# The first norm of a two-block fp32 kernel: two weight units interleaved three tiles apart, and the sum of squares moved to GpSimd

## The reference

```python
def rmsnorm(x, g):
    xf = x.astype(jnp.float32)
    y = xf * lax.rsqrt(jnp.mean(xf * xf, axis=-1, keepdims=True) + NORM_EPS)
    return (y * g.astype(jnp.float32)).astype(x.dtype)
...
h = rmsnorm(x, g_pre)
proj = h @ w_in
u, q, k, v, o, gi, gf, ga, gb = jnp.split(proj, IN_SPLITS, axis=-1)
y_a = jax.nn.gelu(s5_ssm(u, lam_re, lam_im, b_re, b_im, c_re, c_im, d, log_dt))
```

## Time and profile before

| what | value |
|---|---|
| median of 3 runs | 1600.15 us (1598.99 to 1601.24) |
| the profiled execution's own time | 1595.28 us |
| span in the profile, first to last instruction | 1593.1 us |
| mean granted TensorE clock | 0.978 of full speed |
| TensorE busy | 1501.2 us, 94% |
| VectorE busy | 856.4 us, 54% |
| ScalarE busy | 619.7 us, 39% |
| GpSimd busy | 290.2 us, 18% |

### The profile page before, as it was taken

The page is one execution under the profiler, slowest core; times in us unless marked ns, Lnnn a source line. Parts: engine busy times, 40 slices in busy tenths (PEclk is TensorE's granted clock), DMA queues, the critical chain, the costliest instruction groups (busy, mean ns, idle before and its releaser), DMA issues.

```text
span 1593.1 us, 23438 instructions
## 1 busy us (share of the span) xinstructions
PE 1501.2 (94%) x9205; PEld 1294.8 (81%) x9205; DVE 856.4 (54%) x1252; ACT 619.7 (39%) x916; POOL 290.2 (18%) x284
## 2 busy tenths in 40 slices
PE   7698999999979999999996989999979999999998
PEld 7697999999968988988984767887767788888887
DVE  6869744457465443543556446767553533434354
ACT  5447656642243221231234235555452423223130
POOL 2934100000045513631534000000010000000000
PEclk9899999999989999999998999999899999999999
DMA  5121212124202232232231211111112222323221
GB/s 187 54 68 53 68 54 67 54 80 147 93 27 94 92 106 82 91 105 93 89 110 53 93 40 54 41 41 40 40 53 80 88 98 93 105 82 104 93 93 66
DMA packets 35493, 126.17 MB, mean 79 GB/s; under 512 B 4396, under 2 KB 4524, under 8 KB 35280
## 3 DMA queue, kind: packets, MB, share of 16 engines
q1 hardware_dynamic: 33888, 120.09, 22.7%
q10 hardware_dynamic: 864, 4.33, 0.7%
q0 software_dynamic: 656, 0.56, 0.1%
HBM read 122.84 MB, written 2.10 MB: 78 GB/s over the span
## 4 chain that ended last, share of the span: by engine, by line
PE 86%; DVE 8%; ACT 3%; issue 2%; POOL 2%; DMA 0%; SPq 0%; DVEq 0%; ACTq 0%; POOLq 0%
PE ps L1573 72%; PE ps L1903 2%; PE ps L1593 2%; PE ps L1929 2%; PE ps L1751 1%; PE ps L1916 1%; PE ps L1701 1%; PE ps L1884 1%; DVE w_lo L778 1%; PE ps L1634 1%; DVE b_tmp L781 1%; POOL acc L1440 1%; POOL conv_tmp L1531 1%; DVE sq L790 1%; POOL gate_conv L1440 0%
## 5 line engine op out<-in xcount | busy, mean ns | idle before, releaser
L1573 PE MATMUL ps<-h_hi,w_hi 128*128 128x264 f32 (+1 forms) x1792 | 525.0, 342 | 35.2 <-DVE h_lo L790 24.8
L1573 PE MATMUL ps<-h_lo,w_hi 128*128 128x264 f32 (+1 forms) x1792 | 504.9, 330 | 0.0
L1573 PE MATMUL ps<-h_hi,w_lo 128*128 128x264 f32 (+1 forms) x1792 | 503.6, 330 | 0.0
L778 DVE TENSOR_TENSOR w_lo<-w_raw,w_hi 128x1024 fp32r<-128x1024 f32 x223 | 289.7, 1299 | 184.1 <-ACT w_hi L325 182.9
L1573 PEld LDWEIGHTS ps<-h_hi,w_hi 128*128 128x128 f32 x1792 | 306.3, 189 | 84.3 <-issue 36.5
L1573 PEld LDWEIGHTS ps<-h_lo,w_hi 128*128 128x128 f32 x1792 | 303.2, 189 | 36.6 <-issue 7.7
L1573 PEld LDWEIGHTS ps<-h_hi,w_lo 128*128 128x128 f32 x1792 | 303.0, 189 | 31.3
L325 ACT ACTIVATE w_hi<-w_raw 128x1024 fp32r<-128x1024 f32 x223 | 232.8, 1051 | 229.2 <-PE ps L1573 228.2
L1573 PE MATMUL ps<-mlp_lo,w_hi 128*128 128x512 f32 x256 | 100.9, 394 | 0.0
L1573 PE MATMUL ps<-mlp_hi,w_hi 128*128 128x512 f32 x256 | 100.3, 392 | 0.0
L1573 PE MATMUL ps<-mlp_hi,w_lo 128*128 128x512 f32 x256 | 99.4, 388 | 0.0
(11 more groups left out here) (283 smaller groups left out, 1939.1 us busy)
## 6 DMA issues: line engine op xcount, KB each, us to landing
w_raw<-w_units SPq DMA_DIRECT2D x223, 512.0 KB, 3.7
x<-x_t ACTq DMA_DIRECT2D x1, 2112.0 KB, 8.1
out<-out_tile SPq DMA_DIRECT2D x8, 256.0 KB, 2.0
x<-x_t ACTq DMA_DIRECT2D x3, 528.0 KB, 9.1
x<-x_t ACTq DMA_DIRECT2D x2, 264.0 KB, 4.5
dil<-dil POOLq DMA_DIRECT2D x1, 512.0 KB, 3.6
consts<-consts SPq DMA_DIRECT2D x1, 320.0 KB, 6.9
b_step<-ssm_b SPq DMA_DIRECT2D x1, 256.0 KB, 10.5
```

Source lines behind the costliest of these rows:

```text
L778: Dv.do(v.tensor_tensor(wlo[:, s % RING, :], raw[:, s % RING, :], f32(whi[:, s % RING, :]), ALU.subtract), lo_ready)
L1573: ins = mm(o, wt[:, s % RING, w], xt[:, kx, c0:c0 + n], start=(b == 0 and a == 0), stop=(b == len(blocks) - 1 and a == 2))
```

## The change

1. Norm 0 moves from the first kind to the second: `PRE, POST` become `(2, 4, 5), (0, 1, 3)`. ACT's `entry_square` writes tile 0's square to `acc`, the others to `sq`, and from tile 3 on waits for POOL's addition of tile m - 2. POOL runs `post_norm(0, T1)` after its clearing and before the small load's scaling; it ends there after six additions. TensorE makes two column sums after the units in place of eight between the blocks.
2. Unit 1 is split after tile 2 and not after tile 5, on ACT and on DVE.
3. TensorE runs units 0 and 1 together: the blocks of unit 1 follow those of unit 0 at a distance of `ENTRY_LAG = 3` tiles. In the order of the program: unit 0 on tiles 0, 1, 2, 3, unit 1 on tile 0, unit 0 on tile 4, unit 1 on tile 1, and so on to unit 0 on tile 7 and unit 1 on tiles 4 to 7; then the two column sums.
4. The counts of the other norms are adapted (a term of `y_scaled` is lowered by one norm).

```diff
-PRE, POST = (0, 2, 4, 5), (1, 3)
+ENTRY_LAG = 3
+PRE, POST = (2, 4, 5), (0, 1, 3)
...
+            def entry_square(m, src):
+                if m >= 3:
+                    act.wait_ge(sem("sq_added"), m - 2)
+                A.do(dn.activation(sq[m % 2][:, :] if m else acc[:, :], src, ACT.Square), sem("sq_ready"))
...
-                tile_square(0, m, x[:, m, :])
-                if m == 5:
+                entry_square(m, x[:, m, :])
+                if m == 2:
                     split_hi(1)
...
-                if m == 5:
+                if m == 2:
                     split_lo(1)
...
+                if norm == 0:
+                    return
                 pool.wait_ge(sem("rs_ready"), norm + 1)
...
             Po.do(g.memset(c_pow[:, :, :, :, :], 0.0), sem("zeros"))
+            post_norm(0, T1)
             pool.wait_ge(sem("ssm_c_in"), 16)
...
+            def block_of(s, xhi, xlo, outs, k):
+                for a, (wt, xt) in enumerate(((whi, xhi), (whi, xlo), (wlo, xhi))):
+                    for o, c0, n in outs:
+                        ins = mm(o, wt[:, s % RING, k * P:k * P + P], xt[:, k, c0:c0 + n], start=(k == 0 and a == 0),
+                                 stop=(k == KT - 1 and a == 2))
+                return ins
+
+            def two_units(s, outs, ready, base, lag, after):
+                begin(s)
+                for k in range(KT + lag):
+                    if k < KT:
+                        pe.wait_ge(ready, base + k + 1)
+                        ins = block_of(s, hhi, hlo, outs[0], k)
+                        if k == KT - 1:
+                            ins.then_inc(unit_done, 1)
+                        after(k)
+                    if k == lag:
+                        begin(s + 1)
+                    if k >= lag:
+                        ins = block_of(s + 1, hhi, hlo, outs[1], k - lag)
+                        if k - lag == KT - 1:
+                            ins.then_inc(unit_done, 1)
...
             for n in range(U_GLU):
-                begin(n)
+                if n > 1:
+                    begin(n)
                 if n == 0:
-                    unit(n, 0, hhi, hlo, halves(n), sem("h1_lo"), after=lambda b: tile_sum(0, T1, b))
-                else:
+                    two_units(0, (halves(0), halves(1)), sem("h1_lo"), 0, ENTRY_LAG, lambda k: None)
+                    post_stat(0, T1)
+                elif n > 1:
                     unit(n, 0, hhi, hlo, halves(n))
```

More of the change, by code:

```diff
@@ L1143, in residual @@
                         else:
-                            dve.wait_ge(sem("y_scaled"), (KT - OWN_SCALED) * POST.index(norm) + m - OWN_SCALED + 1)
+                            dve.wait_ge(sem("y_scaled"), (KT - OWN_SCALED) * (POST.index(norm) - 1) + m - OWN_SCALED + 1)
                         stt(x[:, m, c0:T1], ysum[:, m, 0:n], col(gain, m), x[:, m, c0:T1], M, A_, sem(ready))
```

## The result

The changed kernel took 1606.76 us, the median of 20 runs, beside 1599.15 us for the kernel before in runs of the same kind. The medians are 7.6 us apart; the ratio, estimated from all undisturbed runs and not from the two medians, is 1.0038 with a 95% interval of 1.0025 to 1.0051: slower by 6.1 us (4.0 to 8.2). One of the 20 runs of before took 5250.62 us, which its median hardly feels. I had forecast 2.4 us, from the one start of `rs`. That start did become late, and by more than 2.4 us. But in the medians and in the profiled execution there is a second part, far from the change, that the prediction does not contain.

A forecast was written before the change was run, and what follows sets the result against it. The prediction took the chain through DVE from the first `rs` operation as the bound, with TensorE slack behind it. `rs` moves from 24.25 to 26.7 us, giving 1600.15 + 2.4 = 1602.5 us; range 1599.8 to 1606.0 us.

The forecast's parts named there:

- TensorE has slack from 24 to 69 us, and one start decides: Entry to transposes: the chain runs through DVE and ACT, so only the first `rs` operation's start, 24.25 us, matters.
- rival 2: Between 24 and 69 us: TensorE sets the pace, so units done earlier make it 3.3 us faster; chance 0.05.
- unit 1's blocks, which nobody needed yet, stand ahead of the sums: TensorE before `rs`: six saved sums, 5.4 us, are spent on unit 1's blocks, 5.8 us; alone +0.5 us.
- the lower bound: Entry: if `hlo` of tiles 4 to 7 always comes in time, `rs` starts at 25.55 us, 1.3 us later.
- the feed: Entry: DVE's `hlo` supply to TensorE, slowed by GpSimd's additions taking turns, puts `rs` at 26.7 us, +2.4 us.
- pitch of 1.76 us: Entry, tiles 4 to 7: one GpSimd addition and one `hlo` together take 1.76 us, read from norm 1.
- complete turns of 2.08 us: Entry: addition and `hlo` never overlap, 2.08 us a pair, putting `rs` at 28.0 us, +3.7 us.
- the term before it: Entry, before the turns: tile 3's `hlo` runs without an addition beside it, 0.77 us, and is there at 14.2 us.
- rival 1: Entry: the feed is slower still or TensorE's clock falls in the new pause; +3.2 to +4.1 us, chance 0.20.
- a delay has nothing to be lost in: From `rs` to the kernel's end: each step waits for the one before, so the full +2.4 us reach the end.

The follow-up runs named there:

- e3: Changed kernel with the two column sums moved ahead of unit 1's blocks on tiles 4 to 7; ratio to the kernel before 1.0016.
- e4: Changed kernel with GpSimd's six additions cut to one column of 528; ratio to the kernel before 1.0032.
- e5: Kernel before with only units 0 and 1 interleaved and unit 1 split at tile 2, column sums still between blocks on TensorE; ratio 1.0045.
- e6: Kernel before with only the squares added on GpSimd, units in old order, and unit 1 split after tile 7 instead of tile 5; ratio 1.0002.
- e12: Changed kernel with ten unused matmuls filling TensorE's pause before unit 0's block on tile 3; ratio to the kernel before 1.0065.
- e9: Changed kernel run once more unaltered, as control for the runs with a delay; median 1607.74 us, ratio to the kernel before 1.0066.
- e11: Changed kernel with four extra DVE multiplications, 3.0 us of delay, behind the first norm's factor; median 1603.64 us, ratio to the kernel before 1.0032.
- e7: Changed kernel with two extra DVE multiplications, 1.5 us of delay, behind the first norm's factor; median 1601.34 us, ratio to the kernel before 1.0027.
- e10: Repeat of e7, the changed kernel with 1.5 us of delay; median 1602.44 us, ratio to the kernel before 1.0031.
- e1: Kernel before with five extra DVE multiplications, some 3.7 us of pure delay, behind the first norm's factor; ratio to the kernel before 1.0002.
- e2: Kernel before with only the squares added on GpSimd, units in old order and unit 1 split at tile 5; ratio 1.0013.

## Why the prediction was right or wrong, point by point

**Right: TensorE has slack from 24 to 69 us, and one start decides.** In the profile after `rs` is 3.70 us late and the transposes 3.67 us. In e3, e4, e5 and e6 `rs` moved by +0.5, +1.15, +2.9 and -0.85 us against before, and the transposes by +0.4, +1.1, +2.8 and -0.9 us. From `rs` to the transposes it is 44.6 to 44.7 us in all nine profiles without a delay. TensorE still waits 11.4 us before the transposes. The unit that was done 4 us earlier (26.1 us, before 30.0 us) brought nothing; rival 2 is out. The slack shrank, though: unit 2 ended at 41.7 us, not at the 37.7 or 39.4 us of the prediction, since TensorE paused 4.8 us and then ran slowly up to 38.4 us; DVE came for it at 45.67 us.

**Right in kind: unit 1's blocks, which nobody needed yet, stand ahead of the sums.** The prediction says so, and e3, in which only that order is undone, shows what the last four of them cost: 2.9 us by their price, 3.2 us measured.

**Right: the lower bound.** 25.55 us foretold for a feed without turns, 25.40 us in e4, by two errors of 0.4 and 0.3 us that nearly cancel.

**Right in kind, mis-sized: the feed.** The pitch of 1.76 us for an addition and an `hlo`, read from norm 1, is the measured one (1.75 us in e12). The complete turns of 2.08 us, which the rule of the Trainium skill, "SBUF — State Buffer", section "SBUF: two separate sides", gives when taken at its word, do not occur: 1.75 us for a pair whose members take 1.31 and 0.77 us alone. What was mis-sized is the term before it. I let tile 3's `hlo` run alone, since its addition was due 0.05 us after the subtraction's end. In the profiled execution the addition came first by 0.03 us, and tile 3 was there at 15.0 us, not 14.2 us. With tile 3 in the turns only three more follow, for tile 7's `hlo` has no addition beside it (0.90 us), and TensorE has seven blocks left at tile 6: 15.0 + 3 x 1.75 + 7 x 0.73 + 1.8 = 27.2 us, where e12 measured 27.41 us. The low level behind the pause adds 0.4 us to that, 27.8 us, and the changed kernel measured 27.95 us. Where the order fell the other way (e9) it was 26.68 us, against 26.7 us in the text, and that agreement is luck: tile 3 was there 0.5 us earlier than foretold, and the blocks then ran slowly up to 16.6 us.

By size, the +3.7 us of the first profile lie outside the 1.3 to 3.2 us of my forecast for `rs` and inside rival 1. That they equal the +3.7 us of the complete turns is luck, too, since the pitch was 1.75 us.

**Rival 1 happened in part.** The pause before tile 3 was 2.12 us. The clock was low behind it in the changed kernel (up to 17.9 us), in e9 (up to 16.6 us, pause of 1.18 us) and in e11 (up to 22.0 us, `rs` at 30.18 us), and not in e7 (pause of 2.11 us, full speed at once). The time from TensorE's restart to `rs` gives the price: 12.87, 12.94 and 14.39 us against 12.45 us in e7. So it was 0.4 us in the changed kernel, since the feed takes back the rest, and 1.9 us in e11. The prediction had 0.8 to 1.7 us for it. In e10 the blocks were at full speed for 1.3 us and slow only then, from 16.2 us to 19.4 us.

**The step that failed: "a delay has nothing to be lost in", the +2.4 us go through to the end.** Up to the transposes that holds. Behind them it does not, in either direction. e1 carries 3.7 us of delay and is at 1.0002; e7 and e10 add 1.5 us and are 5 us faster than the changed kernel. Behind the transposes the chain passes several pauses of TensorE, and near 1112 us the clock fell behind one of 2.5 to 2.7 us in five profiles and not in nine. That decides over more than the change at the entry: 6.3 us at that place alone. The prediction looked at the clock only at the entry, and took the kernel before as one number though its runs, too, lie 10 us apart. The measured 6.1 us are, by an estimate from the lists of runs, some 3.5 us from the entry (the fastest runs of both are 3.3 us apart, the profiled `rs` 3.7 us) and the rest from a larger share of runs in the low-clock group. They are more than the 5.85 us by which the top of my range lies over the median of before, with an interval that reaches below it, and slower by more than 0.2% had a chance of only 0.24.

**What stays open.** All kernels with the two units interleaved and no added delay have half or more of their runs in the low-clock group: 17 of 26, 6 of 12, 5 of 10, 7 of 12, and 5 of 5 in e12. Those with the old order have few: 8 of 84, 0 of 12, 2 of 12, 2 of 11 and 0 of 11. The transposes of the two kinds overlap (69.35 us in e3, 70.03 us in e2), so the share does not hang on that one time alone. What in the interleaved order sets it, between the entry and 1112 us, was not found. In the changed kernel a new pause of 4.8 us and a slow unit 2 stand between 27 and 69 us, but the group does not need them: e3's profiled run is in it, with a pause of 1.88 us and TensorE at full speed from 18 to 59 us. That the group comes with that order, and all but disappears with 1.5 us of delay (1 of 14 runs against 17 of 26), is shown. Why is not, nor whether the delay or the two extra multiplications do it.

## What to carry to other kernels

Before giving an engine work early, look at what stands behind it in the engine's own list: four blocks of a unit that nobody needed held back a sum that everybody waited for, and in e6 two low parts that nobody needed yet held back `rs` by 1.1 us. A GpSimd addition next to a DVE operation with two SBUF inputs cost DVE time here though nobody waited for GpSimd: an `hlo` with an addition beside it went from 0.77 to about 1.8 us. When a change moves a start by a few microseconds in a kernel whose TensorE pauses, compare runs at like mean clock as well as the medians, and add a pure delay to either kernel: if a delay makes it faster, part of the difference is how the clock happens to fall in later pauses, and no count of the change's own work will explain it. One profile of each kernel is not enough: here the same entry differed by 1 us and more between executions.

## What the runs showed of the hardware

The granted clock of the profile did not show the slow start at the entry: it reads 1.00 from 9 to 13 us in the changed kernel, where two matmuls take 0.64 us, and 0.41 us later on. At the entry the durations have to be read, not that column.

```profile
9.00:13.00 4.00, 3.96 (x18) 3.65 (x17) 2.66 (x3) 3.29 (x6) 2.97 (x2) 1.00 1.03 417
```

The same pause of 2.50 to 2.52 us in front of the same ten matmuls (line 1916 before, 1953 after) led to a granted clock of 0.57 over the next 16 us in the changed kernel and to 1.00 in the kernel before. In the kernel before the clock did fall at the second such place, behind a pause of 2.52 us as well (at 1133.76 us). The length of a pause did not tell whether the clock fell.
